# Two broadcast rows and one early weight piece requested ahead of the token gathers of the expert layers

## The reference, cut to what matters

```
x_lat = _layernorm(DN_ALPHA * x_lat + mod_l[:, :, 2] * y_l, ln_g[l, 0], ln_b[l, 0])
h_l = x_lat * (1.0 + mod_l[:, :, 4]) + mod_l[:, :, 3]
...
gsel = jnp.argmax(glog, -1)
top_p, top_i = lax.top_k(jax.nn.softmax(elog_sel, -1), TOP_K_IN_GROUP)
eid = gsel[:, None] * EXPERTS_PER_GROUP + top_i
...
a = jnp.einsum("nd,edf->nef", hf, w_gate)
u = jnp.einsum("nd,edf->nef", hf, w_up)
hid = jax.nn.silu(a) * u * comb[..., None].astype(h.dtype)
return jnp.einsum("nef,efd->nd", hid, w_down).reshape(B, T, D)
...
x_lat = _layernorm(DN_ALPHA * x_lat + mod_l[:, :, 5] * _hier_moe(h_l, *moe_args), ln_g[l, 1], ln_b[l, 1])
```

## Time and profile before

| | |
|---|---|
| median of 3 runs | 1167.3 us (1166.11 to 1167.33) |
| the profiled execution, its time | 1165.15 us |
| its span | 1163.4 us |
| PE busy | 1077.5 us (93%) |
| DVE, ACT, POOL busy | 547.9, 350.0, 97.8 us |
| read from HBM, written | 320.64 MB, 6.88 MB |
| layer 0: six loads of the first pair, gathers, second pair begins | from 276.18, from 310.88, at 345.7 us |
| layer 1: the same | from 818.68, from 853.16, at 887.0 us |

### The profile page before, as it was taken

One profiled execution on the slowest core, in us unless ns is written; L12 is line 12 of the kernel. 1 busy time (PEld: TensorE's weight loads), 2 busy tenths in 40 slices (PEclk: granted clock), 3 DMA queues, 4 the chain that ended last, 5 costly groups with the idle time before them and its releaser, 6 DMA issues.

```text
span 1163.4 us, 14032 instructions
## 1 busy us (share of the span) xinstructions
PE 1077.5 (93%) x4666; PEld 485.1 (42%) x4696; DVE 547.9 (47%) x1244; ACT 350.0 (30%) x600; POOL 97.8 (8%) x169
## 2 busy tenths in 40 slices
PE   6999999999889999999969999999978999999995
PEld 3444534434533333333335645654642333333332
DVE  2373231327654655555664222313764455555645
ACT  1352321312442222222233434331353222222213
POOL 4000000003420000000031000000520000000000
PEclk9999999999899999999989999999879999999998
DMA  9994448493698999999842323212577999999963
GB/s 371 420 391 163 190 190 308 176 413 134 257 389 340 404 401 412 406 388 399 325 177 113 128 72 118 77 53 98 217 278 319 359 381 416 410 398 419 408 244 122
DMA packets 51305, 328.08 MB, mean 282 GB/s; under 512 B 6144, under 2 KB 8784, under 8 KB 14528
## 3 DMA queue, kind: packets, MB, share of 16 engines
q1 hardware_dynamic: 44672, 299.92, 64.7%
q0 software_dynamic: 4832, 20.68, 4.7%
q10 hardware_dynamic: 1760, 6.94, 1.5%
HBM read 320.64 MB, written 6.88 MB: 282 GB/s over the span
## 4 chain that ended last, share of the span: by engine, by line
PE 65%; DMA 19%; DVE 8%; ACT 3%; issue 3%; SPq 1%; DVEq 0%; POOL 0%; ACTq 0%; POOLq 0%
PE bank L758 33%; DMA ring<-in_w_moe 16%; PE bank L1219 15%; PE bank L1256 5%; PE bank L1236 4%; PE bank L784 2%; DMA ring<-in_w_out 1%; DVE zT L1895 1%; PE bank L1271 1%; DMA region<-h_store,toki 1%; PE bank L1196 1%; PE bank L1245 1%; DMA tiny<-in_tiny 1%; SPq L504 1%; DVE lstat L1898 1%
## 5 line engine op out<-in xcount | busy, mean ns | idle before, releaser
L1219 PE MATMUL bank<-ring,region 128*64 128x512 f32 x976 | 225.4, 596 | 13.9 <-DMA ring<-in_w_moe 10.8
L758 PE MATMUL bank<-ring,hT 128*128 128x512 f32 x336 | 148.1, 596 | 0.0
L1219 PEld LDWEIGHTS bank<-ring,region 128*64 128x64 f32 x976 | 72.8, 137 | 136.1 <-issue 134.7
L1256 PE MATMUL bank<-region 128*128 128x512 bf16 x510 | 115.0, 379 | 5.3 <-issue 4.5
L1236 PE MATMUL bank<-ring,region 128*64 128x512 f32 x512 | 116.5, 598 | 0.9 <-ACT region L1761 0.9
L1771 ACT ACTIVATE region<-region 128x512 bf16<-128x512 f32 x60 | 37.7, 630 | 200.4 <-DVE region L2351 200.4
L758 PEld LDWEIGHTS bank<-ring,hT 128*128 128x128 f32 x336 | 62.8, 190 | 77.9 <-issue 76.8
L758 PE MATMUL bank<-ring,region 128*128 128x512 f32 x192 | 85.4, 597 | 5.0 <-ACT region L1719 1.6
L1256 PEld LDWEIGHTS bank<-region 128*128 128x128 bf16 x540 | 50.4, 98 | 81.6 <-issue 22.7
L2351 DVE TENSOR_TENSOR region<-bank,region 128x512 f32<-128x512 f32 x60 | 41.3, 691 | 86.6 <-PE bank L1236 86.5
L758 PE MATMUL bank<-hT,ring 128*128 128x384 f32 x224 | 77.5, 499 | 1.2 <-DMA ring<-in_w_in 1.2
(11 more groups left out here) (344 smaller groups left out, 1285.6 us busy)
## 6 DMA issues: line engine op xcount, KB each, us to landing
ring<-in_w_moe SPq DMA_DIRECT2D x195, 1024.0 KB, 8.9
ring<-in_w_mod SPq DMA_DIRECT2D x42, 1024.0 KB, 11.2
ring<-in_w_in SPq DMA_DIRECT2D x21, 1024.0 KB, 8.0
region<-in_w_mod SPq DMA_DIRECT2D x5, 1024.0 KB, 13.7
ring<-in_w_out SPq DMA_DIRECT2D x4, 1024.0 KB, 7.5
ring<-in_w_out SPq DMA_DIRECT2D x8, 512.0 KB, 7.0
region<-gate_store POOLq DMA_DIRECT2D x4, 1024.0 KB, 7.7
region<-in_lnrows POOLq DMA_DIRECT2D x4, 1024.0 KB, 10.9
```

The costliest lines, as they stand in the source:

```text
L758: ins = pe.matmul(out, lhsT, rhs, start=start, stop=stop, skip_group_check=True)
L1219: ins = pe.matmul(bank[6][u * CAP:(u + 1) * CAP, :], xs[:, k, u * CAP:(u + 1) * CAP], places[u][:, at:at + 2 * DE], start=k == 0, stop=k = ...
L1256: ins = pe.matmul(bank[2 * t + y][:, :], onehot[:, t * P:(t + 1) * P], part[:, c], start=False, stop=False, skip_group_check=True)
```

## The change

Two calls move and one wait is new. On POOL, `bring_rows(2 * l + 1)` now stands ahead of `gather_rows(l)` in both layers. On SP, the load of `early_up[2]` stands ahead of the wait for the gathered rows; in layer 0 it waits for `ranks` (by which time PE has used the piece of another matrix that lies in `st0`), in layer 1 only for what it waited for before.

```diff
@@ SP
                 up_weights(0)
                 down_weights(0)
 
+                sp.wait_ge(S["heads_done"], l + 1)
+                if l == 0:
+                    sp.wait_ge(S["ranks"], 1)
+                sp.wait_ge(landed[0][1], 16 * (g0 // G + 1))
+                sp.dma_start(early_up[2], A["w_moe"][(l * NE + G) * 3 + 1]).then_inc(landed[0][1], 16)
+
                 sp.wait_ge(S["x_new"], NT * (2 * l + 1))
...
                     sp.dma_start(early_up[u], A["w_moe"][(l * NE + G + u) * 3]).then_inc(landed[u][0], 16)
-                sp.wait_ge(S["heads_done"], l + 1)
-                sp.wait_ge(landed[0][1], 16 * (g0 // G + 1))
-                sp.dma_start(early_up[2], A["w_moe"][(l * NE + G) * 3 + 1]).then_inc(landed[0][1], 16)
-
@@ POOL
                 affine(2 * l)
+                bring_rows(2 * l + 1)
                 gather_rows(l)
                 if l == 0:
-                    bring_rows(1)
                     store_gate(1, 1)
...
-                else:
-                    bring_rows(3)
```

## The result

The changed kernel takes 1172.72 us in the median of 22 runs (1167.04 to 1181.85), the kernel before 1166.14 us over its 22 runs beside it: ratio 1.0055, 95% interval 1.0036 to 1.0074, that is 6.4 us slower (4.2 to 8.6). The profiled execution of the changed kernel has a span of 1167.1 us against 1163.4. Single executions of one kernel differ by more than the effect (1159.3 to 1174.9 us for the kernel before), so intervals carry the verdicts in this study, and the traces are read for distances inside one execution, not for their spans.

What follows compares the result with a forecast made beforehand. PE holds 65% of the chain and the gathers' start sets the first pair; 2.4 us of gather delay less 0.6 given back makes +1.8 us, 1169.1 against the median of 1167.3, range 1165.0 to 1171.6.

Steps and rivals of the forecast that it cites:

- What the change adds: Ahead of the gathers, 3 MB beside the h_store stores delay them 1.1 us (layer 0) and 1.3 (layer 1), together 2.4.
- the sum of DMA work beside the stores: Weights, broadcasts, stores and state piece added in time order: stores end at 311.3 in layer 0, 853.8 in layer 1.
- the two bounds: Gather delay per layer: 0 if stores are preferred; all of it last and slower, +1.9 in layer 0, +2 in layer 1.
- That the broadcasts and the piece gain nothing where they were: Behind the gathers, broadcasts had 7.8 us slack before DVE's L2346, and the state piece was not late: gain 0.
- That the freed stretch brings no lead: 7.7 us of DMA work leave 311 to 352, but the queue runs empty afterwards, so no lead is kept: 0.
- rival "faster": Weight stream keeps a lead behind the gathers; about a third of PE's 10.8 us waits goes: 1163.7 us, chance 0.08.
- The gathers wait for the stores: Stores land after the token list, so gathers start at 312.0 and 854.5 in place of 310.88 and 853.16.
- What is given back: Later gathers have more transposes at 2.4 GHz: 0.3 us per layer, 0.6 together (between 0 and 1.2).
- the slow rival: Half clock lasts into the first pair's matmuls, 1171.2 us, or semaphores land late, 1170.3; chance 0.20 for both.
- They take turns by the packet, not by bytes: At the DMA engines, stores with 4 KB rows get less than their share beside 8 KB rows and end nearly last.
- the case that I used as lower bound: Layer 0 stores preferred over all others end by 308 to 308.7, under the list's 310.10, and cost 0.
- The rule on semaphores: Stores' semaphore lands only after each DMA engine's earlier writes across queues; added delay near 3.0 us instead of 2.4.

## Why the prediction was wrong

It forecast +1.8 us, no difference that can be told, and the change costs 6.4. The place and the mechanism were right, the sign too; the step that failed is the sum of DMA work beside the stores, under "What the change adds", and with it the two bounds. The sum had the last store landing at 311.3 in layer 0, and it landed at 314.65: the broadcasts moved fewer bytes per us than I took, and the last store's packets trailed behind the bulk of the work, for which the sum had no term. The cover of that store was also smaller than I read.

**That the broadcasts and the piece gain nothing where they were: right.** With the stores left out the two orders take the same time within 0.2%. DVE's first reader of the rows still waits for ACT, as in the earlier trace rows:

```profile
342.33 0.42 DVE L2346 TENSOR_TENSOR region<-region,bank 128x256 f32<-128x256 f32 x1 [3.11 <-ACT region L1757]
```

**That the freed stretch brings no lead: right as far as it can be told.** PE's waits for weights at L1219 are 9.1 us in 14 places and 11.9 in 16 in the two traces of the change, against 10.8 in 17 and 9.6 in 15 in those of the kernel before, and the pair without stores shows no gain in time. The rival "faster" is out.

**The gathers wait for the stores: right; its size was not.** "Gather at 312.0 in place of 310.88, +1.1 us" was 314.93, and 5.6 us more behind the list; "+1.3 us" in layer 1 was 2.3 to 2.7 (3.1 and 3.5 less 0.8). The terms:

- Work by the megabyte is not contradicted in layer 0, but hardly tested. From POOL's norm to the last store's landing (the gather's start less 0.28 us) it is 17.3 and 18.9 us in the two traces of the change, 15.9 with one broadcast less and 15.8 with the piece later: 1.4 to 3.1 us for each megabyte, where I had 2.6, and two traces of one kernel alone differ by 1.6.
- The rate was too high. I took 405 to 418 GB/s from stretches in which weights or stores ran. While the broadcasts ran in layer 0 it was 317 GB/s at a share of 0.92 (300 to 306). Over 6 us that is 1.4 us of work more.
- More of the first pair's weights was left than I had. The queue of SP still moved 1.29 MB after 297 (1.19 in 297 to 300, 0.10 in 300 to 306), where I had 355 GB/s for 3 us, 1.07 MB: 0.5 us more.
- Nothing in my sum stood for the tail of the stores. The windows have the work done at about 313.3, if it is counted as spread evenly over the 16 engines, but store packets still move, at a share that falls from 0.37 to 0.04, until about 314.2, and the landing is at 314.65: 1.4 us. In the second trace the tail is longer: between 313.5 and 315.0 the share is 0.04 to 0.06, as much as a single engine of 16, and the store lands at 315.28. The trace of the kernel before already had such a tail. Its last store of layer 0 landed after 3.8 us, with packets until about 308.5:

```profile
DMA to landing us min/median/max: 2.6/2.7/3.8
```

Rate, weights and tail are together 3.3 us, which is the difference between 311.3 and 314.65. (POOL's first broadcast starts 0.6 us after its norm and not at once; that cost nothing, since the engines had weights to move until then, at a share of 0.95 in 297 to 300.) The rest of layer 0's 4.5 us is the list: it was ready at 308.55 instead of 310.05, 1.5 us earlier, because this execution had no low clock ahead of it (1.00 in 294 to 297, 0.60 in the kernel before), while the broadcasts hang on POOL, whose norm ended at 297.3 in both. Against it, the gather started 0.28 us behind the landing, and not 0.78. The cover was wrong from the start, too: I gave the last store of layer 0 the median of six, 2.8 us. With its own 3.8 us it landed at 309.0 and not at 308.0, and its cover was 1.1 us and not 2.1. And it is no fixed number: the list came 12.8 and 15.6 us behind POOL's norm in the two traces of the kernel before, and 11.2 in both of the change.

In layer 1 the rate was right (424 and 392 GB/s in the windows 846 to 850 and 850 to 855), and so was the work: it ends 14.0 us behind the norm, as in my sum, if counted evenly. Only the tail was missing: the last store packets are seen up to 858.7, and the landing came 15.3 us behind the norm. The state piece was issued at 303.55 and 840.50, where I had 305.1 and 836.

My upper bounds, +1.9 and +2, were my sum and "a little slower"; they were no bounds. An honest upper end adds the tail to everything and takes the lowest rate that a trace shows.

**What is given back: wrong.** I expected the gathers' delay to fall out of the low clock, 0.6 us in both layers together. From the first gather to the second pair it is 35.6 and 33.9 us in layer 0 (34.8 and 34.3 before) and 33.4 and 33.9 in layer 1 (33.9 and 33.9 before): nothing that two traces can show is given back. In the first trace of the change the clock was still at 0.50 (1.2 GHz) in the window 324 to 328, where the kernel before had 1.00 (2.4 GHz); in the second it was at 1.00 there, though PE had been idle still longer ahead of it. So the later gathers do not fix where the clock rises. The first two rows are the first trace, the last two the second:

```profile
313.00:324.00 11.00, 4.56 (x19) 3.36 (x18) 5.22 (x17) 2.22 (x4) 7.55 (x8) 0.50 0.64 193
324.00:328.00 4.00, 3.66 (x16) 3.13 (x16) 0.00 (x0) 1.90 (x4) 0.46 (x1) 0.50 0.80 278
...
313.00:324.00 11.00, 3.80 (x16) 3.14 (x16) 4.07 (x15) 1.86 (x4) 6.92 (x8) 0.53 0.56 173
324.00:328.00 4.00, 2.71 (x21) 2.28 (x22) 0.03 (x1) 2.70 (x5) 0.48 (x1) 1.00 0.83 329
```

A low clock after 324 was the sign for the slow rival as the prediction put it, but it costs little: in the trace that has it, list to second pair grew by 6.3 us where the gather's start explains 5.6. So the loss is not the clock's.

**The shares: the turns were right, the entry was missing.** "They take turns by the packet, not by bytes" was read from the earlier trace rows, and the changed kernel's trace bears it out for the stretches in which a store's packets run beside others. Packets, MB and share of 16 engines for 302 to 305, then 307 to 310, then 851 to 855 (q0 has the broadcasts, q1 the weights, q10 the stores):

```profile
q0 software_dynamic: 124, 0.91, 97.3%
q10 hardware_dynamic: 2, 0.01, 0.7%
...
q1 hardware_dynamic: 88, 0.72, 56.9%
q10 hardware_dynamic: 105, 0.38, 31.3%
...
q0 software_dynamic: 152, 1.10, 65.3%
q10 hardware_dynamic: 141, 0.54, 33.1%
```

The first two rows show what my sum did not have: the stores were issued from 300.70 on, and up to 305 they had moved two packets. Their packets start 4 to 4.5 us behind the issue of the first store in layer 0 and 3.5 in layer 1, in both traces, where in the kernel before they start within 1 us. In that time no turn was shared. With rows of 4 KB it is the same (about 4 us in layer 0), and the stores land no sooner. Why they enter so late no run shows. The end of the summed work need not move by it, since the engines have other work meanwhile, but it takes away the case that I used as lower bound, stores served ahead of the rest.

The rule on semaphores that I quoted from the Trainium skill, DMA: Bandwidth & Descriptors, section Queues, rings and completion order, explains none of the miss in layer 0. In 313 to 315 the only packets are the stores' own (34 of q10), so none of another queue was in flight to wait for, and the 0.6 us that I had set on it had no row behind it.

**What stays open.** Counted from the list, the excess up to the second pair adds up to 8.8 us in the traces (means of two: 6.5 and 2.3), the time to 6.4 (4.2 to 8.6). Counted from the end of POOL's norm it is 5.0 (53.2 and 53.0 us against 48.4 and 50.7 in layer 0, 49.1 and 49.9 against 47.2 and 49.0 in layer 1). The difference lies in the list, as I read it: the stores' landing hangs on POOL's broadcasts, so where the list comes early the wait behind it is longer, and the second pair is no later for that. In layer 0 the clock of the traces parts between 291 and 297, ahead of the first moved instruction at 297.9. Six of the eight traces with a broadcast right behind POOL's norm in layer 0 have the early list (11.2 us behind the norm), and none of the six others has; why is not known. How much of the loss is the piece's is not settled either: alone it costs nothing that can be measured, the broadcasts alone lose 4.3 us, both lose 6.4, and the intervals overlap. Why the broadcasts of layer 0 run slower is not known. No kernel tried here beats the kernel before: moving the piece alone is level with it.

## What to carry to other kernels

An idle stretch of the DMA engines just ahead of a critical transfer is not free room: here what was put there delayed the small transfer that somebody waited for, from another queue. Before moving a load earlier, look for the smallest store or load on the path beside its new place, take its own landing, not a median of its kind, and its cover over several executions, and sum the DMA work up to the semaphore, the tail included. And ask who waits at the old place: here nobody did, so there was nothing to win.

## What the runs showed of the hardware

- The broadcasts of layer 0 (128 rows of 8 KB, all read from one 8 KB row) ran at 328 and 291 GB/s in two windows of 2 us, in which nearly all packets were theirs, at a DMA share of 0.95 and 0.93; in the kernel before, behind the gathers, at 420 (share 0.99). The second trace of the change has 254 and 319 in the same windows. The first fence is the changed kernel, the second the kernel before.

```profile
301.00:303.00 2.00, 1.53 (x12) 0.98 (x10) 1.68 (x12) 1.50 (x3) 0.00 (x0) 1.00 0.95 328
303.00:305.00 2.00, 1.90 (x13) 1.09 (x14) 1.38 (x6) 1.61 (x3) 0.00 (x0) 1.00 0.93 291
```

```profile
325.00:327.00 2.00, 1.97 (x10) 0.78 (x12) 1.63 (x7) 0.38 (x1) 0.00 (x0) 1.00 0.99 420
```

- Gathers requested right behind two broadcasts on the same queue took 7.4 us to land in layer 0 and 6.0 to 6.1 in layer 1; in the kernel before it was 4.3 to 6.2 and 4.7 to 6.2, in its second trace 6.0 and 6.1 to 6.2.
- A store of 512 KB issued while broadcasts fill the DMA engines moved its first packets 3.5 to 4.5 us after its issue in the two traces of the change, against less than 1 us in the kernel before; from then on it took turns by the packet with the other queue (141 packets against 152 in 851 to 855).
- In layer 0 of the kernel before the last of the three stores landed after 3.8 us, and after 4.0 in its second trace, the others after 2.6 to 2.9.
